# Two blocks on one core: the first block's attention regrouped into four rounds of head pairs

## The chip, the core and the metric

One core of a Trainium2 chip runs the whole program. The metric is the device time of one execution in microseconds. Everything is in fp32. The profile shows every matmul product as two records, so a product of two accumulation steps appears as four records. Engines are named as in the profile: PE is TensorE (PEld its weight loads), DVE is VectorE, ACT is ScalarE, POOL is GpSimd and SP is SyncE, whose queue issues the weight loads.

## What is computed

Two model blocks run one after the other on 256 tokens of width 1024. Block 1 has two layers, each with a convolution branch, a neighbourhood attention with 8 heads of 64 channels, an output projection and a feed-forward part (dense in layer 0, eight experts with two chosen per token in layer 1). Block 2 has two layers of windowed attention and a recurrent part, and is steered by a condition vector. Only this part of the reference bears on the change:

```python
# block 1, layer i
conv_out = conformer_conv(a, g, conv_w[i], conv_b[i], conv_ln_g[i], conv_ln_b[i])
attn_out = neighbourhood_attention(q, k, v, rpb[i])   # per head: softmax(q k^T * scale + bias, masked) v
mix = jnp.concatenate([conv_out, attn_out], axis=-1) @ w_out[i] + b_out[i]
h = layer_norm(DEEPNORM_ALPHA * h + mix, ln1_g[i], ln1_b[i])
# block 2, layer l: its modulation depends on the conditions alone
mod_x = jnp.split((sc @ w_ada[l] + b_ada[l])[:, None, :], 3, axis=-1)
mod_c = jnp.split(scc @ w_ada[l] + b_ada[l], 3, axis=-1)
```

The condition product `sc @ w_ada[l]` needs nothing of block 1, so the kernel computes it beside block 1's attention.

## The kernel before

Each engine has its own program, written out by hand, and semaphores order them. Activations are kept with features on partitions and 256 tokens on the free axis. Weights come as 471 units of 1 MB each (128 partitions by 2048 numbers), loaded by SP in the order of use into a ring of six slots. A slot is loaded again when TensorE has released its unit: `next_unit` waits for a unit and, unless it is called with `beside=True`, marks all units held so far for release; the next product (`mm`, L463) carries the release. A unit taken `beside` others is held together with them.

PSUM has eight banks of 512 numbers per partition. `fill` (TensorE) waits until the bank's last reader is done; `tile` (the readers) waits until the bank is full.

One layer of block 1 is: projection (10 units), then the attention stage, then `block1_out` (the attention half of the output projection, 2 units), then the norm and the feed-forward part. In layer 1 the experts follow; which experts' units are loaded is read from the routing's result by SP.

The attention stage mixes four kinds of work on TensorE.

- A condition row (`condition_row`): one unit of `w_ada`, eight products with a stationary operand of 32 columns in four column groups, 256 columns moving. ScalarE copies the row out of PSUM (L1556) into `cond_row`, which has two places. Layer 0 has 12 rows, layer 1 has 8.
- A turn of a row (`condition_turn`): two products with two moving columns, which sum the four groups and put the row on partitions. It waits for ScalarE's copy.
- Attention: the scores of head i are two products with 64 rows of the array (L627), head i in row half i % 2 and bank 2 + i % 2. VectorE adds bias and mask (L2148) and takes the negative maximum (L2151), ScalarE takes the exponentials (L1635) and their sums, VectorE scales by the reciprocal sum (L2137, L2139), TensorE transposes the weights (L641, four transposes), ScalarE copies them (L1629), and TensorE multiplies by the values (L650): two products with 64 columns, head h in column half h % 2 of bank 6. ScalarE copies a pair's output (L1626). `prob1` has three places, `pt1` two.
- The convolution half of the output projection (`conv_half`): 8 output chunks, each of four accumulated products of full width into bank 7. ScalarE reads each with a bias (L1640), VectorE adds the residual (L2155). One unit holds the weights of four chunks.

In the loop over i, TensorE does: row i + 3 and turn of row i + 2, scores of head i, chunk i - 1, transposes of head i - 2, output of head i - 3. Three rows come ahead of the loop. ScalarE's Silu of the convolution branch (L1617), which the chunks need, stands behind its three row copies. `mixed_order` gives the order of the units of rows and chunks, from which the host lays out the weights.

Of the kernel before, what the change touches and what calls it, by code (L numbers as in the profile page):

```python
# [108 lines left out]

def mixed_order(l):  # L110

    rows = [("row", u) for u in range(l * ADA_EARLY, UNITS_ADA)]
    order, rows = rows[:4], rows[4:]
    for i in range(1, HEADS + 1):
        order += rows[:1]
        rows = rows[1:]
        if i % 4 == 1:
            order.append(("half", i // 4))
    return order + rows
# [66 lines left out]
def build(nc, weights, params, consts, x_t, ctx_t, p_t, rel, out):  # L186
    with ExitStack() as ctx:
# [50 lines left out]
        prob1, pt1 = cut(3, TT, T), cut(2, TT, T)  # L238
# [4 lines left out]
        cond_s = cut(KC, 32)  # L243

# [191 lines left out]
        def _(eng):  # L436
# [130 lines left out]
            half_open = [False]  # L567

            def condition_row(l, u, bank):
                w = next_unit(beside=half_open[0])  # L570
                o = fill(("row", l, u), bank, (s["cond_row"], UNITS_ADA * l + u + 1))
# [3 lines left out]
                last.then_inc(bank_full[bank], 1)  # L575

            def condition_turn(l, u, mod_t):
                eng.wait_ge(s["cond_row"], UNITS_ADA * l + u + 1)
                for half in range(2):
                    at = 2 * (2 * u + half)  # L580
                    last = mm(mod_t[:, at:at + 2], cond_row[:, u % 2, half * P:half * P + P],
                              con[:, CN("fold", 0, 2)], True, True)
                return last

            def conditions(l):


                eng.wait_ge(s["cond_ready"], 1)
                mod_t = fill(("mod", l), 0, (s["mod_out"], 2 * l + 1))
                for u in range(l * ADA_EARLY, UNITS_ADA + 1):  # L590
                    if u < UNITS_ADA:
                        condition_row(l, u, 1)
                    if u > l * ADA_EARLY:
                        last = condition_turn(l, u - 1, mod_t)
                    if u == UNITS_ADA:
                        last.then_inc(bank_full[0], 1)
                    yield
# [15 lines left out]
            def block1_attention(l, filler):  # L613
                eng.wait_ge(s["qk_out"], CC * (l + 1))
                eng.wait_ge(s["v_out"], 2 * (l + 1))
                for i in range(HEADS + 3):
                    half_open[0] = 1 <= i <= HEADS and i % 4 != 1
                    if i % 4 == 2 and half_open[0]:
                        release[0] += held[0] - 1
                        held[0] = 1  # L620
                    before_row = unit_no[0]
                    next(filler, None)
                    if i < HEADS:
                        b, p0 = 2 + i % 2, DH * (i % 2)
                        o = fill(("s", l, i), b, (s["nbr_scored"], HEADS * l + i + 1))
                        for t in range(TT):
                            last = mm(o[:, t * T:(t + 1) * T], q1[p0:p0 + DH, i // 2, t * P:t * P + P],  # L627
                                      k1[p0:p0 + DH, i // 2, :], True, True)
                        last.then_inc(bank_full[b], 1)
                    if 1 <= i <= KC:  # L630
                        if i % 4 == 1:
                            w = next_unit(beside=unit_no[0] > before_row)
                        conv_half(l, i - 1, w)
                    if 2 <= i < HEADS + 2:
                        h = i - 2
                        b = 4 + h % 2
                        eng.wait_ge(s["nbr_prob"], HEADS * l + h + 1)
                        o = fill(("pt", l, h), b, (s["nbr_turned"], HEADS * l + h + 1))
                        for t in range(TT):
                            for kt in range(TT):  # L640
                                last = eng.transpose(o[:, kt * T + t * P:kt * T + t * P + P],  # L641
                                                     prob1[:, h % 3, t, kt * P:kt * P + P], ident)
                        last.then_inc(bank_full[b], 1)
                    if i >= 3:
                        h = i - 3
                        eng.wait_ge(s["nbr_turned"], HEADS * l + h + 1)
                        if h % 2 == 0:
                            o2 = fill(("o", l, h // 2), 6, (s["nbr_out"], CC * l + h // 2 + 1))
                        for kt in range(TT):
                            last = mm(o2[DH * (h % 2):DH * (h % 2) + DH, 0:T],  # L650
                                      v1[:, kt, h * DH:h * DH + DH], pt1[:, h % 2, kt, :], kt == 0, kt == TT - 1)
                        if h % 2 == 1:
                            last.then_inc(bank_full[6], 1)

            def conv_half(l, c, w):

                if c == 0:
                    eng.wait_ge(s["conv_mixed"], CC * (l + 1))
                o = fill(("half", l, c), 7, (s["mix_biased"], KC * l + c + 1))
                for k in range(CC):  # L660
                    at = k * 4 * P + (c % 4) * P
                    last = mm(o[:, 0:T], w[:, at:at + P], mix1[:, k, :], k == 0, k == CC - 1)
                last.then_inc(bank_full[7], 1)
# [774 lines left out]
            for l in range(DEPTH):  # L1438
                block1_projection(l)
                filler = conditions(l)  # L1440
                for _ in range(3):
                    next(filler)
                block1_attention(l, filler)
                for _ in filler:
                    pass
# [88 lines left out]
        def _(eng):  # L1534
# [23 lines left out]
            def conditions(l):  # L1558
                for u in range(l * ADA_EARLY, UNITS_ADA):
                    condition_row(l, u)  # L1560
                    yield
# [58 lines left out]
            def block1_attention(l, filler):  # L1620
                for i in range(HEADS + 4):
                    next(filler, None)
                    if i >= 5 and i % 2 == 1:
                        h2 = (i - 5) // 2
                        o = tile(eng, "o", l, h2)
                        eng.activation(mix1[:, CC + h2, :], o[:, 0:T], ACT.Copy).then_inc(s["nbr_out"], 1)  # L1626
                    if 3 <= i < HEADS + 3:
                        o = tile(eng, "pt", l, i - 3)
                        eng.activation(pt1[:, (i - 3) % 2].rearrange("p a b -> p (a b)"), o, ACT.Copy)\  # L1629
                            .then_inc(s["nbr_turned"], 1)  # L1630
                    if i < HEADS:
                        k = HEADS * l + i + 1
                        eng.wait_ge(s["nbr_max"], k)
                        for t in range(TT):
                            eng.activation(prob1[:, i % 3, t, :], prob1[:, i % 3, t, :], ACT.Exp,  # L1635
                                           bias=rmax[:, i % 3, t:t + 1], accum_out=rsum[:, i % 3, t:t + 1])\
                                .then_inc(s["nbr_exp"], 1)
                    if 1 <= i <= KC:
                        o = tile(eng, "half", l, i - 1)
                        eng.activation(sq[:, i - 1, :], o[:, 0:T], ACT.Identity, bias=par[:, PC(f"b_out{l}", i - 1)])\  # L1640
                            .then_inc(s["mix_biased"], 1)
# [316 lines left out]
            for l in range(DEPTH):  # L1958
                block1_projection(l)
                filler = conditions(l)  # L1960
                norm(f"conv{l}", CC, T)
                for _ in range(3):
                    next(filler)
                conv_silu(l)
                block1_attention(l, filler)
                for _ in filler:
                    pass
# [30 lines left out]
        def _(eng):  # L1998
# [132 lines left out]
            def block1_attention(l):  # L2131
                eng.wait_ge(s["rel_ready"], TT * (l + 1))
                for i in range(HEADS + 2):
                    if i >= 2:
                        h = i - 2
                        eng.wait_ge(s["nbr_exp"], 2 * (HEADS * l + h + 1))
                        link(eng.reciprocal(rinv[:, h % 3, :], rsum[:, h % 3, :]))  # L2137
                        for t in range(TT):
                            ins = eng.tensor_scalar(prob1[:, h % 3, t, :], prob1[:, h % 3, t, :],  # L2139
                                                    rinv[:, h % 3, t:t + 1], None, ALU.mult)  # L2140
                        ins.then_inc(s["nbr_prob"], 1)
                    if i < HEADS:
                        k = HEADS * l + i + 1
                        pr = prob1[:, i % 3]
# [959 lines left out]
```

## Time and profile before

| | us |
|---|---|
| median of the runs shown (3) | 2128.38 |
| lowest and highest | 2126.7, 2137.03 |
| the profiled execution | 2130.35 |
| its span, first to last instruction | 2128.6 |
| attention stage of layer 0, first row to `block1_out` (96.49 to 152.03) | 55.54 |
| attention stage of layer 1 (498.96 to 548.72) | 49.76 |

Times in the rows are microseconds from the start of the span. In a row of the order of time stand the start, the length of a merged run of equal instructions, the engine, the line, the operation, the tiles, the shape and the count; in brackets how long the engine was idle before it and what ended that. A merged run's length reaches to its last record's end, which overlaps the start of the next run, so the cost of a run on TensorE is read from its start to the next run's start.

### The profile page before, as it was taken

What the parts mean: (1) busy time and instruction counts of PE and PEld (TensorE: products, weight loads), DVE (VectorE), ACT (ScalarE), POOL (GpSimd) and SP (SyncE); (2) the same over time, 40 slices, a digit from 0 to 9 for tenths busy, and PEclk for the clock granted to TensorE, in tenths of its full rate; (3) what the DMA queues carried; (4) which work ended last, traced back from release to release, by engine and by line L of the source; (5) the groups of instructions that cost most, each with busy time, mean ns of one, the idle gap of its engine ahead of it and who ended that gap; (6) DMA issues with size and microseconds to landing.
All of it is one profiled execution on the core that took longest, in us unless ns stands there. A gap on an engine that the chain in (4) does not pass through costs nothing.

```text
span 2128.6 us, 36866 instructions
## 1 busy us (share of the span) xinstructions
PE 2036.4 (96%) x15858; PEld 1470.3 (69%) x15858; DVE 790.8 (37%) x1796; ACT 406.6 (19%) x964; POOL 5.7 (0%) x12
## 2 busy tenths in 40 slices
PE   8999999999999999999999999998999999999887
PEld 6879999987776656666666566665744667474776
DVE  5737555595521111111011101112336354346454
ACT  1232110103310111000000000001133333023322
POOL 0000000000000000000000000000000000000000
PEclk9999999999999999999999999999999999999999
DMA  9464445444189999999999999995211111131120
GB/s 316 175 242 176 159 165 193 176 176 163 47 349 390 420 420 417 420 420 420 421 418 420 420 419 418 420 414 231 79 60 40 60 40 40 60 119 60 40 80 20
DMA packets 72372, 506.74 MB, mean 238 GB/s; under 512 B 7824, under 2 KB 9872, under 8 KB 11792
## 3 DMA queue, kind: packets, MB, share of 16 engines
q1 hardware_dynamic: 71056, 500.15, 58.6%
q0 software_dynamic: 1152, 4.19, 0.9%
q8 instruction: 128, 2.10, 0.4%
q14 instruction: 36, 0.29, 0.0%
HBM read 503.27 MB, written 1.05 MB: 237 GB/s over the span
## 4 chain that ended last, share of the span: by engine, by line
PE 87%; DMA 6%; DVE 3%; ACT 2%; issue 1%; SPq 0%; DVEq 0%; ACTq 0%
PE ps L463 85%; DMA work<-weights 4%; DMA ring<-weights 2%; PE ps L1225 1%; PE ps L778 1%; DVE work L2696 1%; ACT work L1844 0%; DMA xc<-x_t 0%; DVE work L2657 0%; PE ps L641 0%; DVE work L2763 0%; DVE work L2653 0%; PE ps L1326 0%; DVE work L2654 0%; ACT work L1617 0%
## 5 line engine op out<-in xcount | busy, mean ns | idle before, releaser
L463 PE MATMUL ps<-work 128*32 128x256 f32 (+8 forms) x5608 | 585.5, 382 | 22.7 <-DVE work L2708 6.3
L463 PE MATMUL ps<-work,ring 128*128 128x256 f32 (+2 forms) x2056 | 525.6, 409 | 7.2 <-DVE work L2763 5.0
L463 PEld LDWEIGHTS ps<-work 128*32 128x32 f32 (+3 forms) x5608 | 378.7, 138 | 187.4 <-issue 110.3
L463 PE MATMUL ps<-ring,work 128*32 128x256 f32 (+3 forms) x4824 | 469.0, 410 | 13.5 <-DMA work<-weights 3.8
L463 PEld LDWEIGHTS ps<-work,ring 128*128 128x128 f32 x2056 | 350.9, 191 | 149.2 <-issue 111.9
L463 PEld LDWEIGHTS ps<-ring,work 128*32 128x32 f32 (+1 forms) x4824 | 260.1, 119 | 147.7 <-issue 76.3
L463 PE MATMUL ps<-xc,ring 128*128 128x256 f32 (+1 forms) x1440 | 276.6, 352 | 5.6 <-DMA ring<-weights 4.0
L463 PEld LDWEIGHTS ps<-xc,ring 128*128 128x128 f32 x1440 | 241.4, 191 | 42.4 <-issue 6.7
L2309 DVE TENSOR_TENSOR work<-work,ps 128x256 f32<-128x256 f32 x42 | 17.7, 422 | 421.0 <-ACT work L1688 421.0
L463 PE MATMUL ps<-xc,work 128*128 128x256 f32 (+1 forms) x720 | 138.3, 350 | 0.0
L463 PEld LDWEIGHTS ps<-xc,work 128*128 128x128 f32 x720 | 120.8, 191 | 19.9 <-issue 3.8
L1688 ACT ACTIVATE work<-ps 128x256 f32<-128x256 f32 x42 | 16.2, 385 | 576.5 <-PE ps L463 576.5
L2083 DVE SCALAR_TENSOR_TENSOR work<-work,par 128x256 f32<-128x256 f32 x240 | 98.0, 486 | 0.9
L2271 DVE TENSOR_TENSOR work<-ps,work 128x512 f32<-128x512 f32 x68 | 47.1, 692 | 92.3 <-PE ps L463 92.0
L463 PE MATMUL ps<-work,con 128*128 128x256 f32 x230 | 58.1, 399 | 11.7 <-ACT work L1546 5.6
L463 PEld LDWEIGHTS ps<-work,con 128*128 128x128 f32 x230 | 44.1, 198 | 24.2 <-issue 11.9
L2430 DVE TENSOR_TENSOR work<-ring 128x512 f32<-128x512 f32 x52 | 33.6, 688 | 51.6 <-PE ps L463 51.6
L463 PEld LDWEIGHTS ps<-con,work 128*128 128x128 f32 x336 | 42.4, 190 | 13.3 <-issue 8.2
L463 PE MATMUL ps<-con,work 128*128 128x128 f32 (+2 forms) x336 | 45.0, 267 | 2.8 <-DVE work L2654 2.8
L2323 DVE TENSOR_TENSOR work<-work 128x512 f32<-128x512 f32 x14 | 9.7, 692 | 97.6 <-ACT work L1696 97.6
L2609 DVE SCALAR_TENSOR_TENSOR work<-work,par 128x512 f32<-128x512 f32 (+1 forms) x64 | 39.8, 679 | 0.0
L1734 ACT ACTIVATE work<-ps 128x256 f32<-128x256 f32 x52 | 20.0, 384 | 103.1 <-PE ps L463 103.1
(277 smaller groups left out, 1186.0 us busy)
## 6 DMA issues: line engine op xcount, KB each, us to landing
ring<-weights SPq DMA_DIRECT2D x317, 1024.0 KB, 13.0
work<-weights SPq DMA_DIRECT2D x154, 1024.0 KB, 16.6
work<-rel POOLq DMA_DIRECT2D x8, 512.0 KB, 7.8
con<-consts SPq DMA_DIRECT2D x1, 1368.0 KB, 21.6
xc<-x_t SPq DMA_DIRECT2D x1, 1024.0 KB, 7.8
xc<-ctx_t SPq DMA_DIRECT2D x1, 1024.0 KB, 26.1
out<-work SPq DMA_DIRECT2D x4, 256.0 KB, 2.1
par<-params SPq DMA_DIRECT2D x1, 872.0 KB, 9.2
```

The costliest lines, as they stand in the source:

```text
L463: ins = eng.matmul(o, lhs, rhs, start=start, stop=stop, **kw)
L778: last = eng.transpose(o[:, k * P:k * P + P], pair_a[:, n % 2, k * P:k * P + P], ident)
L1225: last = eng.transpose(o[:, kt * P:kt * P + P], prob2_flat[:, at:at + P], ident)
L1688: eng.activation(pair_s[:, n % 2, :], o[:, 0:GW], ACT.Silu).then_inc(s["pair_silu"], 1)
L1734: eng.activation(snap[n % 2][:, at:at + T], o[:, 0:T], ACT.Copy).then_inc(s["snap_out"], 1)
L2083: ins = eng.scalar_tensor_tensor(out=conv_acc[:, j, :], in0=src, scalar=w, in1=conv_acc[:, j, :], op0=ALU.mult, op1=ALU.add)
L2271: return eng.tensor_tensor(r, o.rearrange("p (a b) -> p a b", b=T), r, ALU.add)
L2309: eng.tensor_tensor(pair_a[:, n % 2, :], pair_s[:, n % 2, :], o[:, GW:2 * GW], ALU.mult)\
L2323: eng.tensor_tensor(v, v, rows(gate_row, 2), ALU.mult).then_inc(s["first_weighted"], 1)
L2430: ins = eng.tensor_tensor(up_sum(i, z), in0, in1, op)
L2609: ins = eng.scalar_tensor_tensor(out=acc, in0=src, scalar=w, in1=acc, op0=ALU.mult, op1=ALU.add)
L2696: ins = eng.scalar_tensor_tensor(out=state[:, n, :], in0=state[:, n, :], scalar=wt_pair[:, j % 2, 1, n:n + 1], in1=o[:, h * 129:h * 129 + ...
```

## The change

The loop over 8 heads becomes a loop over four rounds of two heads.

- Scores: for each of the two query tiles the two heads' products alternate, head 2r in row half 0 and bank 2, head 2r + 1 in row half 1 and bank 3.
- Outputs: for each key tile the two heads' products alternate in the two column halves of bank 6.
- Rows: two units fill the two halves of one bank, ScalarE copies both with one instruction of 512 columns, and the turns of two rows follow each other. `cond_row` and a new `other_row` alternate. `ROW_ROUNDS` says in which rounds rows are drawn: ahead of the loop (-1), in rounds 0 to 3 and behind the loop (4) in layer 0; at -1, 0, 2 and 4 in layer 1.
- Chunks: two output chunks fill one bank (`half_pair`).
- `prob1` has two places in place of three. A pair's scores, softmax and transposes lie in one round, its output in the next.
- ScalarE's first row copy stands behind the Silu. TensorE's first turns stand behind the first scores and the second rows.

The order on TensorE in round r: scores of pair r, output of pair r - 1, two rows (where drawn), in round 0 the first turns, two chunks, two turns (where drawn), transposes of pair r. After round 3: two rows, the last output, the last turns.

The diff, cut to its core:

```diff
-            def conditions(l):
-                eng.wait_ge(s["cond_ready"], 1)
-                mod_t = fill(("mod", l), 0, (s["mod_out"], 2 * l + 1))
-                for u in range(l * ADA_EARLY, UNITS_ADA + 1):
...
+            def condition_rows(l, n, beside=False):
+                u = l * ADA_EARLY + 2 * n
+                bank = 1 if n else 5
+                o = fill(("row", l, u), bank, (s["cond_row"], UNITS_ADA * l + u + 2))
+                for k in range(2):
+                    w = next_unit(beside=beside or k == 1)
+                    for c in range(KC):
+                        at = 32 * (c % 4)
+                        last = mm(o[at:at + 32, k * GW:(k + 1) * GW], cond_s[:, c, :], w[:, c * GW:(c + 1) * GW],
+                                  c < 4, c >= KC - 4)
+                last.then_inc(bank_full[bank], 1)
...
-            def block1_attention(l, filler):
+            def block1_attention(l):
+                eng.wait_ge(s["cond_ready"], 1)
+                condition_rows(l, 0)
                 eng.wait_ge(s["qk_out"], CC * (l + 1))
                 eng.wait_ge(s["v_out"], 2 * (l + 1))
...
+                for r in range(HEADS // 2 + 1):
+                    drawn = ROW_ROUNDS[l].index(r) if r in ROW_ROUNDS[l] else None
+                    if r == HEADS // 2:
+                        condition_rows(l, drawn)
+                    if r < HEADS // 2:
+                        for k in range(2):
+                            h = 2 * r + k
+                            fill(("s", l, h), 2 + k, (s["nbr_scored"], HEADS * l + h + 1))
+                        for t in range(TT):
+                            for k in range(2):
+                                p0 = DH * k
+                                last = mm(ps[:, 2 + k, t * T:(t + 1) * T], q1[p0:p0 + DH, r, t * P:t * P + P],
+                                          k1[p0:p0 + DH, r, :], True, True)
+                                if t == TT - 1:
+                                    last.then_inc(bank_full[2 + k], 1)
+                    if r:
+                        eng.wait_ge(s["nbr_turned"], HEADS * l + 2 * r)
+                        o2 = fill(("o", l, r - 1), 6, (s["nbr_out"], CC * l + r))
+                        for kt in range(TT):
+                            for k in range(2):
+                                h = 2 * r - 2 + k
+                                last = mm(o2[DH * k:DH * k + DH, 0:T], v1[:, kt, h * DH:h * DH + DH], pt1[:, k, kt, :],
+                                          kt == 0, kt == TT - 1)
+                        last.then_inc(bank_full[6], 1)
+                    if r % 2 == 1:
                         release[0] += held[0] - 1
                         held[0] = 1
...
+                    if drawn is not None and r < HEADS // 2:
+                        condition_rows(l, drawn, beside=r % 2 == 1)
+                    if r == 0:
+                        mod_t = fill(("mod", l), 0, (s["mod_out"], 2 * l + 1))
+                        condition_turns(l, 0, mod_t)
+                    if r < HEADS // 2:
+                        if r % 2 == 0:
+                            w = next_unit(beside=drawn is not None)
+                        half_pair(l, r, w)
+                    if drawn is not None:
+                        condition_turns(l, drawn, mod_t)
...
+                o = fill(("half", l, r), 7, (s["mix_biased"], KC * l + 2 * r + 2))
+                for f in range(2):
+                    for k in range(CC):
+                        at = k * 4 * P + (2 * (r % 2) + f) * P
+                        last = mm(o[:, f * T:f * T + T], w[:, at:at + P], mix1[:, k, :], k == 0, k == CC - 1)
                 last.then_inc(bank_full[7], 1)
```

On ScalarE a round is: output copy of the pair before, exponentials of two heads, one copy of two rows (where drawn), two biased chunks, two copies of transposed weights. On VectorE a round is: bias and maximum of two heads, then reciprocal and scaling of two heads, then two residual additions.

## Rows read from the trace of the kernel before

**Rows 1.** Stretches (both stages): busy PE, PEld, DVE, ACT, POOL; clock, DMA, GB/s

```profile
96.49:152.03 55.54, 53.85 (x401) 35.92 (x400) 23.01 (x54) 26.21 (x70) 2.72 (x4) 1.00 0.69 243
498.96:548.72 49.76, 47.70 (x322) 32.19 (x321) 22.68 (x54) 24.76 (x66) 0.00 (x0) 1.00 0.44 170
```

**Rows 2.** Order of time on PE: one iteration of layer 0's loop

```profile
132.50 1.07 PE L463 MATMUL ps<-ring,work 128*32 128x256 f32 x16
133.50 0.61 PE L463 MATMUL ps<-con,work 128*128 128x2 f32 x4
134.03 1.13 PE L463 MATMUL ps<-work 64*128 64x256 f32 x4
135.09 1.99 PE L463 MATMUL ps<-work,ring 128*128 128x256 f32 x8
136.92 0.60 PE L641 MATMUL ps<-con,work 128*128 128x128 f32 x4
137.45 1.08 PE L463 MATMUL ps<-work 128*64 128x256 f32 x4
138.46 1.07 PE L463 MATMUL ps<-ring,work 128*32 128x256 f32 x16
```

**Rows 3.** PE's order of time: idles in layer 0's prologue and layer 1

```profile
98.16 1.07 PE L463 MATMUL ps<-ring,work 128*32 128x256 f32 x16 [0.59 <-ACT work L1556]
...
105.13 1.07 PE L463 MATMUL ps<-ring,work 128*32 128x256 f32 x16 [1.00 <-ACT work L1556]
...
547.22 1.56 PE L463 MATMUL ps<-work 128*64 128x256 f32 x8 [0.38 <-ACT work L1629]
```

**Rows 4.** Stretches: weights in layer 0's stage and at layer 1's routing

```profile
130.00:140.00 10.00, 10.00 (x75) 6.56 (x73) 4.07 (x11) 4.19 (x14) 0.00 (x0) 1.00 1.00 424
...
575.00:580.00 5.00, 5.00 (x37) 4.63 (x36) 2.26 (x10) 0.90 (x2) 0.00 (x0) 1.00 0.00 0
...
585.00:590.00 5.00, 2.28 (x5) 1.85 (x6) 4.76 (x19) 0.07 (x1) 0.00 (x0) 0.50 1.00 398
```

**Rows 5.** PE's order of time in block 2's attention: row halves, column halves

```profile
1556.86 1.13 PE L463 MATMUL ps<-work 64*128 64x512 f32 x4 [0.19 <-ACT work L1780]
1557.92 3.70 PE L463 MATMUL ps<-work,ring 128*128 128x512 f32 x8
...
1671.01 1.09 PE L463 MATMUL ps<-work 128*64 128x128 f32 x16
```

**Rows 6.** Groups of weight loads by form, layer 0's stage: busy us, mean ns

```profile
L463 PEld LDWEIGHTS ps<-work 128*64 128x64 f32 x32 | 3.7, 136 | 2.6 <-issue 1.0 <-ACT work L1629 0.2
```

**Rows 7.** Order of time on VectorE in layer 0's stage

```profile
98.89 1.43 DVE L2033 TENSOR_TENSOR work<-work 128x256 f32<-128x256 f32 x4
...
129.24 0.69 DVE L2148 TENSOR_TENSOR work<-ps,work 128x512 f32<-128x512 f32 x1 [3.49 <-PE ps L463]
129.96 0.69 DVE L2151 TENSOR_REDUCE small<-work 128x2 f32<-128x512 f32 x1
...
131.09 0.62 DVE L2139 TENSOR_SCALAR work<-work,small 128x256 f32<-128x256 f32 x2
```

**Rows 8.** Order of time on ScalarE in layer 0's stage

```profile
101.34 1.28 ACT L1617 ACT_TABLE_LOAD   x1
102.64 2.08 ACT L1617 ACTIVATE work<-work,par 128x256 f32<-128x256 f32 x4
...
128.22 0.60 ACT L1629 ACTIVATE work<-ps 128x512 f32<-128x512 f32 x1
...
130.68 0.51 ACT L1635 ACTIVATE work<-work,small 128x256 f32<-128x256 f32 x1 [1.86 <-DVE small L2151]
```

**Rows 9.** DMA view, 90 to 165 us: queue and issues (median to landing)

```profile
q0 software_dynamic: 576, 2.10, 13.0%
...
ring<-weights SPq DMA_DIRECT2D x16, 1024.0 KB, 7.6
```

**Rows 10.** Order of time on GpSimd from 95 to 165 us

```profile
142.15 2.72 POOL L1530 DMA_DIRECT2D work<-rel  x4 [105.47 <-DVE work L2148]
```

More of the change, by code:

```diff
@@ L107, in moe_order @@
             yield GATES, EARLY_GATES + GATE_CELLS.index(c)
+ROW_ROUNDS = ([-1, 0, 1, 2, 3, 4], [-1, 0, 2, 4])
 def mixed_order(l):
[L112 to L119, printed above, removed]
+    order, u = [], l * ADA_EARLY
+    for r in range(-1, HEADS // 2 + 1):
+        if r in ROW_ROUNDS[l]:
+            order += [("row", u), ("row", u + 1)]
+            u += 2
+        if r in (0, 2):
+            order.append(("half", r // 2))
+    assert u == UNITS_ADA
+    return order
 def ring_places():
@@ L565, in block1_projection, with row_products @@
                 norm_var(f"conv{l}", CC, T, True, 2)
[L567 to L571, printed above, removed]
+            def row_products(l, u, o):
+                w = next_unit()
                 for c in range(KC):
@@ L574, in condition_row, with turn @@
                     last = mm(o[at:at + 32, 0:GW], cond_s[:, c, :], w[:, c * GW:(c + 1) * GW], c < 4, c >= KC - 4)
-                last.then_inc(bank_full[bank], 1)
+                return last
+            def condition_row(l, u, bank):
+                o = fill(("row", l, u), bank, (s["cond_row"], UNITS_ADA * l + u + 1))
+                row_products(l, u, o).then_inc(bank_full[bank], 1)
+            def turn(u, rows, mod_t):
+                for half in range(2):
+                    at = 2 * (2 * u + half)
+                    last = mm(mod_t[:, at:at + 2], rows[:, u % 2, half * P:half * P + P],
+                              con[:, CN("fold", 0, 2)], True, True)
+                return last
@@ L577, in condition_turn @@
             def condition_turn(l, u, mod_t):
                 eng.wait_ge(s["cond_row"], UNITS_ADA * l + u + 1)
[L579 to L583, printed above, removed]
-            def conditions(l):
-                eng.wait_ge(s["cond_ready"], 1)
-                mod_t = fill(("mod", l), 0, (s["mod_out"], 2 * l + 1))
-                for u in range(l * ADA_EARLY, UNITS_ADA + 1):
[L591 to L597, printed above, removed]
+                return turn(u, cond_row, mod_t)
@@ L630, in block1_attention @@
[L630 to L653, printed above, removed]
@@ L1439, in _ @@
                 block1_projection(l)
[L1440 to L1445, printed above, removed]
+                block1_attention(l)
                 block1_out(l)
@@ L1556, in condition_row, with condition_rows @@
                 eng.activation(cond_row[:, u % 2, :], o[:, 0:GW], ACT.Copy).then_inc(s["cond_row"], 1)
[L1558 to L1561, printed above, removed]
+            def condition_rows(l, n):
+                u = l * ADA_EARLY + 2 * n
+                o = tile(eng, "row", l, u)
+                eng.activation(row_of[n % 2].rearrange("p a b -> p (a b)"), o, ACT.Copy).then_inc(s["cond_row"], 2)
             def context_squares():
@@ L1959, in _ @@
                 block1_projection(l)
[L1960 removed]
                 norm(f"conv{l}", CC, T)
[L1962 to L1963 removed]
                 conv_silu(l)
[L1965 to L1967 removed]
+                condition_rows(l, 0)
+                block1_attention(l)
                 norm(f"ln1_{l}", KC, T)
```

125 lines of the change are left out of this document (67 added, 58 removed).

## Prediction, made before the changed kernel was run

> **What bounds the kernel now.** I read the table of stretches over the two attention stages first, then TensorE in order of time inside them, then the helpers in the same order, then the weight stream. The two stages (block 1's layers 0 and 1) last 55.54 and 49.76 us; TensorE is busy 53.85 and 47.70 of that at full clock, VectorE 23.01 and 22.68, ScalarE 26.21 and 24.76, and the DMA engines 0.69 and 0.44 of the time [rows 1]. The order of time shows the same: in the steady loop every TensorE group starts where the one before it ends, and one iteration takes 138.46 - 132.50 = 5.96 us [rows 2]. From the starts, a condition row costs 1.00, its turn 0.53, a head's scores 1.06, an output chunk 1.83, the four transposes 0.53, a head's output 1.01. So TensorE's own length is the bound here, helpers have slack, and what shortens TensorE's list shortens the program. The exceptions are the idle times: 0.59 and 1.00 us in layer 0's prologue behind ScalarE's copy of a row, the same two in layer 1, and 0.38 before layer 1's last output [rows 3].
>
> Time gained here reaches the end. The expert weights cannot be asked for before the routing: the stream stands still and then fills the DMA engines from 585 us on [rows 4]. So it moves with its start, and so does all that follows.
>
> **Scores on row halves.** The count of products stays. Before, a head's two products are four records that use 64 of 128 rows, one after the other, 1.06 us [rows 2]. After, the two heads of a pair alternate, each in its own row half and its own bank. The trace has this form already, in block 2: two products of 64x512 in the two row halves take 1.06 us to the next start (1556.86 to 1557.92), in four records, while eight full-width records of 128x512 behind them take 3.70 [rows 5]: 0.27 against 0.46 each. Halves therefore run side by side. A pair costs what one head costs: 8 heads x 1.06 become 4 x 1.06 in each layer, -4.24 us a layer.
>
> **Outputs on column halves.** Again block 2 has the form: 16 records of 128*64 on 128 columns take about 1.09 us, 0.07 each [rows 5], against 0.13 each for the full-width transposes on 128 columns (4 in 0.53) [rows 2]. So a pair should cost one head's 1.01: 8 x 1.01 become 4 x 1.01. The last two heads already ran one behind the other without a change of form, 1.50 for both in layer 1 (547.22 to the stage's end) [rows 1, 3], so the gain is 6 x 1.01 + 1.50 - 4 x 1.01 = 3.5; I take -3.6 us a layer, since layer 0's last pair is longer.
>
> One rule speaks against this half. The rows that bear on it: a load of 128*64 takes 136 ns by itself [rows 6], and yet in block 2 the records of such pairs follow each other every 0.07 us, loads included [rows 5]. The Trainium skill ("TensorE: Matmul & The Clock Gate", The mechanism) says that a weight load overlaps a running matmul only when the row groups differ, and column halves share all rows. By that rule each of 4 load steps a round would lie bare, 4 x 0.136 x 8 rounds = 4.4 us of the gain gone; the rows say otherwise, and I leave it a small chance.
>
> **Fewer changes of form.** A group loses some time at its start and end. One record step is 0.216 us in a chunk of 8 (1.83 = 8 x 0.216 + 0.10) and about 0.11 in turns and transposes. Two units in one row group cost 2 x 1.00 - 0.13, two turns 2 x 0.53 - 0.09, two chunks 3.66 - 0.10, two heads' transposes 1.06 - 0.09. Six row pairs in layer 0 and four in layer 1, with four rounds each, give -2.1 and -1.6 us. Bounds: nothing, if the wait for the second unit splits the group as before, to these sums; I take them, since waits already met cost no gap in the steady loop [rows 2].
>
> **The prologue.** Before, three single rows each wait for ScalarE's copy. After, TensorE runs rows (1.87), the first pair's scores (1.06), rows (1.87), and only then the turns. ScalarE now does Silu first. VectorE's four scaled chunks are there from 99.3 to 100.32 [rows 7]; the Silu table load (1.28) was issued only at 101.34 behind the third copy and can now lie beside VectorE's work; four Silu take 2.08 [rows 8]. That gives 99.35 + 2.08 = 101.4, then one copy of 128x512 at 0.60 [rows 8], 0.14 until TensorE starts: 102.1. TensorE arrives at 96.5 + 0.1 + 1.87 + 1.06 + 1.87 = 101.4. So 0.7 us of idle instead of 1.59; the same in layer 1. Bounds: 0.3 to 2.0 (the table load bare). The last output is covered by rows at the end (0.38 gone), but two rounds without rows in layer 1 may show 0.2 each at the output, behind ScalarE's two biased chunks and two copies. I take -0.8 us for each layer.
>
> **What hides the softmax.** The chain of a pair is now shut into one round, with two weight buffers in place of three. From the scores' end, VectorE adds and takes maxima for two heads, 4 x 0.69 = 2.8; the second head's two exponentials take 2 x 0.51; its scaling 0.62 with a reciprocal before it, 0.8; with hand-overs 4.85 us until the second head may be turned [rows 7, 8]. In front of those transposes TensorE has the previous output 1.0, two chunks 3.56 and the first head's transposes 0.5: 5.1. That covers it by 0.25 in the two rounds of layer 1 without rows, and by 3.1 where rows (1.87) and turns (0.97) are drawn. ScalarE's queue in a round is exponentials, row copy, two chunks, two transposed copies; the turns behind the row copy need it by S + 6.4 and get it by S + 4.5 (S: scores' end). So cost nothing, up to 1 us in each of two rounds.
>
> **The weight stream.** The loads behind SP's queue number the same, but units are released in twos and threes, at a row pair's first product. A unit of 1 MB takes about 2.5 us at 424 GB/s [rows 4], and 7.6 from issue to landing in the median, queue included [rows 9]; three released together have landed after about 3 x 2.5 + 2 = 9.5 us (the 2 is an estimate: 7.6 less two units ahead). A round lasts 9.44; the first two of them are due one round later, the third two. Tight spot: POOL's bias loads for layer 1 start when layer 0's last scores are read (142.15 before [rows 10], about 130 after). They hold 13.0% of a window of 75 us, 9.8 us [rows 9], and now share the engines with the two units for the last row and the first output unit. Slowed 1.9-fold, the latter lands about 139 to 141 and is due at 140.2. I take 0.5 us, bounds 0 to 3.
>
> **The sum.** Layer 0: 4.24 + 3.6 + 2.1 + 0.8 - 0.5 = 10.24; layer 1: 4.24 + 3.6 + 1.6 + 0.8 = 10.24. Together 20.5 us, so stages of 45.3 and 39.5 us. The profiled execution took 2130.35 us (span 2128.6 and 1.75 around it); less 20.5 it is 2109.9. The median of the runs shown is 2128.38, 2 lower, so I say 2108.0.
>
> **Rivals.**
> - Late weights: the joint releases leave TensorE waiting for a landing in three or four rounds of layer 0, 1 to 2 us each. For: the DMA engines were full in parts of the stage (424 GB/s) [rows 4]. Against: six slots, and 0.69 mean. 2110 to 2118.
> - The chain shows in the rounds without rows and in the first ones, 0.5 to 1 us each in 6 of 8: 2110 to 2114. The bare loads of the column halves would end in the same place: 20.5 - 4.4 = 16.1, 2112.
> - The halves don't run side by side here (two products of the same half in a row might hold the other back): scores and outputs gain nothing, 20.5 - 15.7 = 4.8: 2123.6. Against: the row and column pairs of block 2 [rows 5].
> - Slower: the helpers' chain becomes the round's length. ScalarE's one queue carries exponentials, row copies, chunks and transposed copies for TensorE; if the chunk product had to wait for the bias reads of the preceding round, its bank's one reader, TensorE's fill would stand behind the chain and not beside it. A round would be 1.06 + 4.85 + 0.97 + 1.3 + 1.0 + 1.87 + 3.56 + 0.97 = 15.6 us against 2 x 5.96 = 11.9, eight rounds +29, less 1.6 of prologue: 2156. It decides when ScalarE reaches those reads later than the next round's chunk; by my order of its queue it ends them about 1.0 us after a chunk (two reads, each of half the width of the 0.60 copy [rows 8]) and the next comes at least 4.5 later. The Trainium skill ("TensorEngine Tiling (Array Packing)", PSUM Bottleneck) warns that after tiling the PSUM copies may be what limits; ScalarE's 26.21 us in a stage of 45 [rows 1] keeps that away.
> - More gain: the prologue idles vanish and the groups' edges shrink further: 2099 to 2103.
>
> **How the numbers follow.** Forecast 0.73 (own range 2103 to 2112), late weights 0.07, the chain 0.05, bare loads 0.02, halves not together 0.05, slower 0.04, more gain 0.04. The clock is full in both stages [rows 1], but 0.50 in a stretch at the routing [rows 4]; moving the program by 20 us may lengthen or shorten such stretches, some 2 us either way, which the range holds. The range 2101 to 2116 takes in the forecast and most of the first two rivals, and leaves out the others, 0.13 or so. A measurement of this kernel can tell about 0.5% (10.6 us) from no change: faster by more than that is all above except halves not together (0.05 to the same, with 0.02 of the latest weights) and slower: 0.89, 0.07, 0.04.
>
> **What would show it.** After: groups of 8 records of 64*128 in 1.06 us and of 128*64 in 1.0; row pairs of 32 records in 1.87; one idle of 0.7 in each prologue behind ScalarE's copy; hardly any between; the routing's idle moved 20 us forward and unchanged behind it. It would be wrong if those groups took 2 us, if TensorE idles before transposes behind VectorE in each round, or if it waits for DMA.

## The result

The changed kernel took 2111.15 us (median of 4 executions, 2109.45 to 2112.75), the kernel before 2132.7 us beside it (4 executions, 2126.7 to 2137.27): a ratio of 0.9901 with an interval of 0.9881 to 0.9921, so 21 us less. That is inside the forecast range, 3 us above the forecast time.

The profiled execution of the changed kernel took 2112.75 us, its span 2111.0, which is 17.6 less than the span before. The two attention stages, in the table of stretches (columns as in [rows 1]):

```profile
100.34:143.87 43.53, 42.83 (x401) 31.28 (x401) 22.93 (x53) 26.03 (x65) 2.77 (x4) 1.00 0.73 260
495.23:533.38 38.15, 37.44 (x321) 27.62 (x321) 22.89 (x53) 24.84 (x63) 0.00 (x0) 1.00 0.60 222
```

They are 12.01 and 11.60 us shorter than in [rows 1], with the same number of records on TensorE (401; 321 against 322) and the same work on VectorE and ScalarE. TensorE's order of time in layer 0's prologue and in one steady round (two runs of scores and outputs that follow each other are merged here, 16 records under the name of the first):

```profile
100.34 1.93 PE L469 MATMUL ps<-ring,work 128*32 128x256 f32 x32
102.21 1.13 PE L469 MATMUL ps<-work 64*128 64x256 f32 x8
103.27 1.93 PE L469 MATMUL ps<-ring,work 128*32 128x256 f32 x32
105.91 1.02 PE L469 MATMUL ps<-con,work 128*128 128x2 f32 x8 [0.70 <-ACT work L1587]
...
121.46 2.15 PE L469 MATMUL ps<-work 64*128 64x256 f32 x16
123.53 1.93 PE L469 MATMUL ps<-ring,work 128*32 128x256 f32 x32
125.40 3.72 PE L469 MATMUL ps<-work,ring 128*128 128x256 f32 x16
128.96 0.95 PE L469 MATMUL ps<-con,work 128*128 128x2 f32 x8
129.77 1.07 PE L681 MATMUL ps<-con,work 128*128 128x128 f32 x8
130.77 2.15 PE L469 MATMUL ps<-work 64*128 64x256 f32 x16
...
140.08 1.93 PE L469 MATMUL ps<-ring,work 128*32 128x256 f32 x32
141.94 1.08 PE L469 MATMUL ps<-work 128*64 128x256 f32 x8
142.96 1.05 PE L469 MATMUL ps<-con,work 128*128 128x2 f32 x8
143.87 7.15 PE L469 MATMUL ps<-work,ring 128*128 128x256 f32 x32
153.52 6.70 PE L469 MATMUL ps<-work,ring 128*128 128x256 f32 x22 [2.50 <-DMA ring<-weights]
```

A round takes 130.77 - 121.46 = 9.31 us, where two iterations took 2 x 5.96 in [rows 2]. Of the 2.6 us, 2.07 are the scores and outputs (2.07 for both, from 4.14), the rest edges of groups: rows 0.13, chunks 0.10, turns 0.25, transposes 0.06. The first pair's scores alone cost 1.06 (102.21 to 103.27), the last pair's output 1.02 (141.94 to 142.96), each for two heads.

The last row is the loss. Layer 0's output projection waits 2.50 us for its second unit of weights, where the kernel before ran its 64 records without a gap:

```profile
152.03 14.08 PE L463 MATMUL ps<-work,ring 128*128 128x256 f32 x64
```

In the changed kernel GpSimd's bias loads for layer 1 start 33.9 us after the stage's start (45.7 in the kernel before [rows 1, 10]), ahead of that unit, which is asked for at 140.73:

```profile
134.24 2.77 POOL L1556 DMA_DIRECT2D work<-rel  x4 [96.93 <-DVE work L2169]
```

The chain of work that ended last names the load, and the table of stretches behind it a lower granted clock:

```profile
140.73 12.75 DMA ring<-weights
```

```profile
145.00:150.00 5.00, 5.00 (x25) 4.38 (x25) 1.91 (x5) 0.00 (x0) 0.00 (x0) 1.00 1.02 253
150.00:155.00 5.00, 2.50 (x9) 1.84 (x8) 1.07 (x3) 0.00 (x0) 0.00 (x0) 0.88 1.02 296
155.00:160.00 5.00, 5.00 (x19) 4.16 (x19) 1.70 (x4) 0.00 (x0) 0.00 (x0) 0.78 1.01 400
```

The unit is the first of three asked for together and took 12.75 us, where the forecast reckoned 2.5 us for a unit and a latency of about 2; the DMA engines are full (1.02) but move only 253 to 296 GB/s. Then TensorE, which had idled 2.5 us, runs part of the next stretches at the lower of its two clocks (1.2 of 2.4 GHz, so the mean falls to 0.88 and 0.78). From the stage's end to the first products on the next norm's squares this costs 20.85 us where it was 16.42 before: 4.4 us given back. Of these 1.7 are the clock (the unit's 32 records take 8.70 us, 153.52 to 162.22, where they take 7.01 in runs that stay at full clock), the rest is the wait.

So the profiled spans differ by: stages -12.01 and -11.60, layer 0's output projection +4.43, the part behind layer 1's stage -2.27, and the start +3.85. The last two are not the change's. Behind layer 1's stage both kernels do the same, and in the eleven profiles on record that part took from 1576.4 to 1583.0 us, with the kernel before (1579.9) in the middle. Before the first attention stage both kernels do the same too, but this execution had a lower clock in its first 25 us:

```profile
10.00:15.00 5.00, 5.00 (x16) 3.75 (x14) 0.00 (x0) 0.00 (x0) 0.00 (x0) 0.66 1.01 423
15.00:20.00 5.00, 2.61 (x6) 2.15 (x7) 3.44 (x15) 4.34 (x10) 0.00 (x0) 0.73 1.01 423
```

The kernel before had 1.00 in both stretches of its profiled execution. Starts of 96.5 to 100.3 us until the first attention stage were seen among all the profiles, for kernels that are equal up to there. What this pair of profiles shows of the change itself is thus 12.01 + 11.60 - 4.43 = 19.2 us.

### The profile page after: what moved, and what is told of

It is laid out like the page before. It is cut to its first block, busy times and chain, and to the rows that moved or that the text cites. A ratio compares the mean times of both kernels' runs of the same rounds, so it can differ in the third digit from the quotient of the medians.

```text
span 2111.0 us, 36869 instructions
## 1 busy us (share of the span) xinstructions
PE 2019.2 (96%) x15858; PEld 1462.9 (69%) x15858; DVE 791.4 (37%) x1796; ACT 405.9 (19%) x954; POOL 5.9 (0%) x12
## 4 chain that ended last, share of the span: by engine, by line
PE 89%; DMA 4%; DVE 4%; ACT 2%; issue 1%; DVEq 0%; SPq 0%; ACTq 0%
PE ps L469 87%; DMA work<-weights 2%; DMA ring<-weights 2%; PE ps L1256 1%; PE ps L809 1%; DVE work L2724 1%; ACT work L1877 0%; DMA xc<-x_t 0%; DVE work L2685 0%; PE ps L681 0%; DVE work L2056 0%; DVE work L2791 0%; DVE work L2681 0%; PE ps L1357 0%; DVE work L2682 0%
## 5 line engine op out<-in xcount | busy, mean ns | idle before, releaser
L469 PE MATMUL ps<-work 128*32 128x256 f32 (+8 forms) x5608 | 570.8, 383 | 21.1 <-DVE work L2736 6.3
L469 PEld LDWEIGHTS ps<-work 128*32 128x32 f32 (+3 forms) x5608 | 369.9, 138 | 186.0 <-issue 109.7
L2637 DVE SCALAR_TENSOR_TENSOR work<-work,par 128x512 f32<-128x512 f32 (+1 forms) x64 | 39.8, 680 | 0.0
```

The lines of the kernel that those rows point to most:

```text
L469: ins = eng.matmul(o, lhs, rhs, start=start, stop=stop, **kw)
L2637: ins = eng.scalar_tensor_tensor(out=acc, in0=src, scalar=w, in1=acc, op0=ALU.mult, op1=ALU.add)
```

## The experiments

Two theories were open on the gain, and two on the loss. On the gain: products in different halves of the array run side by side when the kernel alternates them; or the gain is something else that came with the regrouping. On the loss: GpSimd's bias loads for layer 1, which now start earlier, take the DMA engines from the weights; or units are asked for too late because they are released in threes. Stage lengths below are read in each run's own trace, from the first row product to the first product of the output projection; the changed kernel has 43.53 and 38.15.

**The changed kernel again.**

> The changed kernel again, beside the runs that follow on the same chip. Expected 2109 to 2113 us. Of interest is what varies between executions: the stages should be 43.5 and 38.2 us again, and the first output projection should wait for its second unit of weights again (2.5 us).

Measured: 2108.67 us (6 executions, 2102.95 to 2115.69), ratio 0.9881 (0.9860 to 0.9901) to the kernel before on this chip (2132.58 us). Stages 44.13 (with one gap of 0.5 us that the trace puts to nothing) and 38.14; the wait for the unit 2.0 us, and the stretch from the stage's end to the norm's squares 20.33 us, 3.9 more than before. The loss is there in both profiles of the change, and in the five runs below that leave the bias loads and the condition rows as the change has them the wait is 1.8 to 2.5 us.

**Bias loads later.**

```diff
-                    eng.wait_ge(s["nbr_scored"], HEADS * l)
+                    eng.wait_ge(s["ffn_act"], 2)
                 for r in range(ROWS):
```

> The changed kernel, but GpSimd's bias loads for layer 1 start in the middle of layer 0's feed-forward part, not right behind layer 0's last scores. Theory (the bias loads take the DMA engines from the weights): the 2.5 us wait of layer 0's output projection for its second unit goes, and so does the stretch at half clock behind it, together 4 us: about 2107 us; both stages keep 43.5 and 38.2 us. Rival (the unit is asked for too late, because three units are released together): the wait stays at 1.5 to 2.5 us and the time at 2110 to 2111.

Measured: 2103.62 us (5 executions, 2102.79 to 2104.69), ratio 0.9866 (0.9844 to 0.9887). (The 2107 expected started from 2111.15; from the 2108.67 of this chip it would be 2104.7.) The bias loads start at 220 us. TensorE's order of time in the output projection, and the stretch from the stage's end to the norm's squares:

```profile
139.41 1.05 PE L469 MATMUL ps<-con,work 128*128 128x2 f32 x8
140.33 14.06 PE L469 MATMUL ps<-work,ring 128*128 128x256 f32 x64
154.22 1.38 PE L469 MATMUL ps<-work,con 128*128 128x256 f32 x4
```

```profile
140.33:156.73 16.40, 15.19 (x71) 12.76 (x70) 7.17 (x19) 0.56 (x2) 0.00 (x0) 1.00 0.81 343
```

All 64 records run through, at full clock, and the stretch is back at 16.40 us (16.42 in the kernel before). The release in threes is still there, so the bias loads were needed for the wait. In the DMA view of the same 75 us the median from issue to landing of the weights falls from 8.4 to 6.9 us:

```profile
ring<-weights SPq DMA_DIRECT2D x17, 1024.0 KB, 8.4
work<-rel POOLq DMA_DIRECT2D x4, 512.0 KB, 15.8
```

```profile
ring<-weights SPq DMA_DIRECT2D x17, 1024.0 KB, 6.9
```

```profile
work<-rel POOLq DMA_DIRECT2D x4, 512.0 KB, 7.8
```

The first fence is the changed kernel, the second this one, the third the bias loads in the kernel before. The bias loads themselves took 15.8 us in the median, against 7.8 in the kernel before: both sides lose. The median is 5 us under the changed kernel's; the single executions touch (2102.95 lies among these).

**Bias loads later, first turns behind the first chunks.**

```diff
                         mod_t = fill(("mod", l), 0, (s["mod_out"], 2 * l + 1))
-                        condition_turns(l, 0, mod_t)
...
                         half_pair(l, r, w)
+                    if r == 0:
+                        condition_turns(l, 0, mod_t)
```

> As the run before, and TensorE's first turns stand behind the first two chunks instead of ahead of them. Theory (the 0.7 us idle in each prologue is ScalarE's Silu and copy, which the chunks can cover): the idle shrinks to about 0.25 us, now before the chunks and ended by the Silu, so each stage is 0.5 us shorter, 43.0 and 37.7 us: about 2106 us. Rival (TensorE is in front of ScalarE there whatever it does): the idle stays 0.7 and only its place changes.

Measured: 2105.68 us (6 executions, 2104.33 to 2110.73), ratio 0.9881 (0.9860 to 0.9901). In the trace it does what was expected: stages 43.15 and 37.77, and TensorE's idle in the prologue falls to 0.33 and now ends with the Silu:

```profile
103.61 3.69 PE L469 MATMUL ps<-work,ring 128*128 128x256 f32 x16 [0.33 <-ACT work L1644]
```

0.75 us in all is less than these runs can tell (the medians stand the other way round by 2 us). The lowest median on record is that of the version with only the bias loads moved.

**Scores head by head.**

```diff
-                        for t in range(TT):
-                            for k in range(2):
+                        for k in range(2):
+                            for t in range(TT):
                                 p0 = DH * k
```

> The changed kernel, but the four score products of a pair in the old order: both of the first head, then both of the second. Theory (only neighbouring products in different row halves run side by side): one of four products still overlaps its neighbour, so a pair takes 7 record steps instead of 4, 1.8 us instead of 1.06: +0.65 to 0.75 in each of four rounds, stages of 46.3 and 41.0 us, about +5.5 us in all. Rival (the array sorts the halves out by itself, and the gain came from fewer groups): stages unchanged.

Measured: stages of 43.54 and 38.15 us (2107.75 us, one execution). Nothing changed. TensorE's order of time, the first pair's scores:

```profile
99.36 1.14 PE L469 MATMUL ps<-work 64*128 64x256 f32 x8
100.44 1.93 PE L469 MATMUL ps<-ring,work 128*32 128x256 f32 x32
```

1.08 us for eight records, as with alternation (1.06). The rival's number came out (its reason, fewer groups, is tested two runs further on), and the prediction's reason fell in part: alternating the heads is not what makes the halves run side by side.

**Outputs head by head.**

```diff
-                        for kt in range(TT):
-                            for k in range(2):
+                        for k in range(2):
+                            for kt in range(TT):
                                 h = 2 * r - 2 + k
```

> The changed kernel, but the four output products of a pair in the old order, head by head. Theory: as in the run before, 1.7 us instead of 1.02 for a pair: +0.65 to 0.75 in each of four rounds, stages of 46.3 and 41.0 us. Rival (weight loads of column halves lie bare, so alternating gains little): +0.2 a round, stages of 44.3 and 39.0.

Measured: stages of 43.54 and 38.16 us (2112.31 us, one execution), the last pair's output 1.02 us:

```profile
139.86 1.09 PE L469 MATMUL ps<-work 128*64 128x256 f32 x8
140.88 1.05 PE L469 MATMUL ps<-con,work 128*128 128x2 f32 x8
```

The same again for column halves. Neither the theory (+0.7 a round) nor the rival of bare weight loads (+0.2) came out.

**The heads' scores parted.** A new theory follows from the two runs: what counts is that the two heads' products are neighbours in TensorE's list, in whatever order. In the kernel before, a chunk, transposes, an output, a row and a turn stood between two heads' scores.

```diff
+                        scores(r, 0)          # head 2r: both products
+                        if r == 0:
+                            scores(r, 1)
...
                         last.then_inc(bank_full[6], 1)   # the preceding pair's output
+                        if r < HEADS // 2:
+                            scores(r, 1)
```

> The changed kernel, but in rounds 1 to 3 the preceding pair's output stands between the scores of the two heads. Theory (products in different halves run side by side when they are neighbours in the list, whatever their order within the pair; a group of another form between them parts them): the two heads cost 2 x 1.06 again, +1.06 in each of three rounds: stages of 46.7 and 41.3 us. Rival (the halves' products are sorted out across other groups too, and only the number of groups counts): +0.2 to 0.3 a round, 44.3 and 39.0 us.

Measured: stages of 46.88 and 41.30 us (2114.01 us, one execution), +3.35 and +3.15. Scores, output and scores of a round now take 3.13 us (2.07 before), without a wait:

```profile
505.08 3.20 PE L469 MATMUL ps<-work 64*128 64x256 f32 x16
508.21 3.72 PE L469 MATMUL ps<-work,ring 128*128 128x256 f32 x16
```

The same 16 records, 1.06 us more, with nothing changed but their neighbours. This is the gain's cause for the scores. The outputs were not parted in a run. For them it is inferred from their equal behaviour and from one place of the kernel before: the outputs of layer 1's last two heads stand next to each other in its list, head by head, and took 1.50 us for both [rows 3] instead of 2 x 1.01, although the second head's could start only when ScalarE had copied its weights, at 546.58 + 1.08 = 547.66, 0.44 us after the first:

```profile
546.58 1.08 ACT L1629 ACTIVATE work<-ps 128x512 f32<-128x512 f32 x2
```

The prediction put that difference down to the missing change of form; but from 547.66 to the stage's end is 1.06 us, about a head's output alone, so what was left of the first head's ran beside it.

**One chunk a bank.**

```diff
-                o = fill(("half", l, r), 7, (s["mix_biased"], KC * l + 2 * r + 2))
                 for f in range(2):
+                    o = fill(("half", l, r, f), 7, (s["mix_biased"], KC * l + 2 * r + f + 1))
...
-                last.then_inc(bank_full[7], 1)
+                    last.then_inc(bank_full[7], 1)
```

> The changed kernel, but each output chunk fills the bank by itself, so that the second chunk waits until ScalarE has read the first. Theory (two chunks a bank take ScalarE's queue out of TensorE's way): 0.75 us of idle in a round where ScalarE is free by then, 1.6 to 1.8 us where it is still at the exponentials (round 0, and the two rounds without rows in layer 1): layer 0 +3.8 to 47.3, layer 1 +5.9 to 44.0 us. Rival (ScalarE is always in time): at most +1 in each stage.

Measured: stages of 47.57 and 43.73 us (2117.48 us, one execution), within 0.3 us of the theory. TensorE's order of time in rounds 0 and 1 of layer 0:

```profile
103.14 1.97 PE L469 MATMUL ps<-work,ring 128*128 128x256 f32 x8
106.39 1.99 PE L469 MATMUL ps<-work,ring 128*128 128x256 f32 x8 [1.28 <-ACT work L1668]
...
113.98 1.99 PE L469 MATMUL ps<-work,ring 128*128 128x256 f32 x8
116.54 1.99 PE L469 MATMUL ps<-work,ring 128*128 128x256 f32 x8 [0.56 <-ACT work L1668]
```

The wait is longer where ScalarE is still at the exponentials. The idle shown (3.0 us in layer 0, 4.6 in layer 1) is less than the stages' growth, since a run's modelled end reaches into the gap behind it.

**The condition units one by one.**

```diff
-                o = fill(("row", l, u), bank, (s["cond_row"], UNITS_ADA * l + u + 2))
                 for k in range(2):
+                    o = fill(("row", l, u + k), bank, (s["cond_row"], UNITS_ADA * l + u + k + 1))
...
+                    last.then_inc(bank_full[bank], 1)
```

(On ScalarE, one copy of 256 columns for each row.)

> The changed kernel, but the two units of a row pair fill the bank one after the other, so that the second waits until ScalarE has copied the first. Theory (pairing the units keeps TensorE out of ScalarE's queue, where the copy stands behind the Silu and the exponentials): about +4 us ahead of the loop, +3.4 in round 0, +2.6 in each later round with rows, +0.7 behind the loop: layer 0 near 59, layer 1 near 49 us, so all of layer 0's gain is gone. Rival (the pairing only saves edges of groups): +0.13 a pair, 44.3 and 38.7 us.

Measured: stages of 68.06 and 53.46 us (2147.63 us, one execution beside 2136.37 of the kernel before). The direction is the theory's, the size more than its 59 and 49. The waits are the expected ones, 14.4 us in layer 0 and 9.0 in layer 1 behind ScalarE's copy:

```profile
PE ps L469 <- ACT work L1588: 14.4, 6, 4.2
```

and the lower clock is about the size of the surplus: a mean of 0.85 over 68.06 us is 10 us, and the 43.53 of the changed kernel with 14.4 and 10 comes to 68 (in layer 1 the mean is 0.87). The stretches of this run (the stage, and its first part) and TensorE's order of time there:

```profile
97.14:165.20 68.06, 53.63 (x402) 36.75 (x401) 22.93 (x53) 27.13 (x71) 2.77 (x4) 0.85 0.53 181
100.00:120.00 20.00, 14.45 (x79) 9.38 (x80) 5.11 (x13) 6.85 (x17) 0.00 (x0) 0.66 0.38 144
```

```profile
110.27 1.94 PE L469 MATMUL ps<-ring,work 128*32 128x256 f32 x16 [3.15 <-ACT work L1588]
112.14 1.87 PE L469 MATMUL ps<-con,work 128*128 128x2 f32 x8
113.87 6.67 PE L469 MATMUL ps<-work,ring 128*128 128x256 f32 x16
```

The two chunks that take 3.56 us at full clock took 6.5 (113.87 to 120.37) behind waits of 4.2 and 3.2 us. Pairing the units is thus no matter of saved edges: with the softmax shut into one round, a row that waits for ScalarE waits for the softmax.

**A longer chain.**

```diff
-                        eng.tensor_reduce(rmax[:, h % 4, :], pr, AX.X, ALU.max, negate=True).then_inc(s["nbr_max"], 1)
+                        link(eng.tensor_reduce(rmax[:, h % 4, :], pr, AX.X, ALU.max, negate=True))
+                        eng.tensor_reduce(rmax[:, h % 4, :], pr, AX.X, ALU.max, negate=True).then_inc(s["nbr_max"], 1)
```

> The changed kernel, with each head's maximum taken twice on VectorE, which makes a pair's chain about 1.5 us longer and changes no result. Theory (the chain is covered by 0.25 us in rounds without rows and by about 3 us where rows and turns are drawn): layer 0 stays at 43.5 us, layer 1 shows about 1.2 us in each of two rounds: 40.6 us. Rival (the chain is the round's length): +1.5 a round, 49.5 and 44.2 us.

Measured: stages of 43.53 and 40.81 us (2118.15 us, one execution). Layer 0 is the same to 0.01 us, layer 1 has its 2.66 us in the two rounds without rows. The waits there, and one round in TensorE's order of time:

```profile
PE ps L681 <- DVE work L2179: 1.8, 4, 0.6
```

```profile
506.50 3.72 PE L469 MATMUL ps<-work,ring 128*128 128x256 f32 x16
510.54 0.66 PE L681 MATMUL ps<-con,work 128*128 128x128 f32 x4 [0.32 <-DVE work L2179]
511.79 0.66 PE L681 MATMUL ps<-con,work 128*128 128x128 f32 x4 [0.60 <-DVE work L2179]
```

The chain grew by 1.44 us: in round 1 of layer 1 the second head's scaling ends 7.31 us after the round's first score, 5.87 in the changed kernel. So it is hidden much as worked out: the 1.44 us vanish where rows are drawn, and where they are not, only about 0.1 us of them does (1.33 show in each round).

## Why the prediction held, step by step

- **What bounds it.** Right: TensorE's list is the stages' length, before and after (42.83 busy of 43.53).
- **Scores and outputs.** The sizes were right (2.07 us for both in a round, forecast 1.06 + 1.01; the last output 1.02). (For block 2's 16 records the prediction took the merged length, 1.09 us; start to start, 1671.01 to 1672.03, they cost 1.02, which only strengthens its reading.) The reason was wrong in one part: the prediction put the gain to alternating heads, and held it possible that two products of the same half in a row hold the other back. Head by head gives the same stages to 0.02 us; parting the two heads' scores brings 1.06 us a round back. It is being neighbours that counts. The rule of the Trainium skill on bare weight loads ("TensorE: Matmul & The Clock Gate", The mechanism) would have shown as 0.5 us a round; the traces do not agree with it for column halves, which ran eight records in 1.02 us.
- **Fewer changes of form.** Right, but low for the turns: 0.81 us for two in a round (128.96 to 129.77) against 0.97 worked out. Over the ten row pairs the turns saved 2.6 us (11.07 before and 8.46 after, added up from the starts in both stages) against 0.9 worked out. Two heads' transposes take 1.00 against 0.97.
- **The prologue.** Right to the digit, and by the steps that were forecast (ScalarE's table load lies beside VectorE's work, TensorE waits for the copy behind the Silu): 0.70 us behind ScalarE's copy in layer 0, 0.71 in layer 1. The 0.2 us behind the transposed copies in the rounds without rows did not appear.
- **What hides the softmax.** Right: no wait in any round. The longer chain measured the cover: about 0.1 us in the rounds without rows, where 0.25 was forecast, and at least 1.44 elsewhere, where 3.1 was; how much more was not tried.
- **The weight stream.** The failed step. The 0.5 us taken (bounds 0 to 3) measured 4.4 and 3.9 us in the two profiles of the change: 2.50 and 2.0 us of wait, and a lower clock behind it. TensorE waiting for DMA was one of the prediction's own signs of being wrong. Two things were wrong in the working. It followed the first unit of the output projection, released at round 3, which was in time; the second, released behind the loop with two others, was the late one. And it priced the wait by TensorE's idle alone, without the clock behind it, which cost 1.7 us in four of the seven profiles that have the wait and nothing in the other three. The bias loads were rightly named as what the weights would meet. The median of 2111.15 also lies in the range of the late-weights rival, but what that rival said, waits in three or four rounds of layer 0, did not come: no round waited for a landing.
- **The sum.** Stages: 43.53 and 38.15 against 45.3 and 39.5 forecast, of which 0.5 was for the weights, so 2.6 us better: 1.7 of that are the turns, 0.55 the idle times. The weights were 3.9 us worse. That the total of 20.5 stands beside 19.2 in the profiles and 21.55 between the medians is in part luck, since these two misses have opposite signs. The forecast's range allowed the parts outside the stages some 2 us either way; in the profiles the part behind layer 1's stage varies by 6.5 us and the start by 3.9, whatever the kernel. Against the median that the forecast started from (2128.38 of three executions; 2132.7 with a fourth), the time itself came 3 us later than forecast.
- **The slower rival.** Nothing of it showed in the kernel as built. Kernels close to it lose much all the same, by waits that need only that one of the things that TensorE takes from ScalarE within a round is not paired. One chunk a bank costs 9.6 us in both stages together, single condition units 39.8, which is more than the 23.6 that the change gained there.

## What to carry to other kernels

In this kernel products that use half of the array's rows or columns gained when their partners stood next to them in the list; their order within that group made no difference here. Where a helpers' chain is shut into one round of an engine's list, look at whatever that engine takes from the same helpers in the round: here rows and chunks had to be buffered two at a time, or TensorE waited for ScalarE behind the chain. A stage that gets shorter moves up every load that is started by its progress: look up what those loads will meet, and price a wait of TensorE with and without a lower clock behind it.

## What the runs showed of the hardware that was not expected

- Products of two heads in one half each need not alternate: eight records took 1.08 us head by head and 1.06 alternating for row halves, 1.02 both ways for column halves.
- With the bias loads running, the DMA engines were full (1.02) at 253 to 296 GB/s in the two stretches shown, between an estimate of the bias loads' own rate (2.10 MB in 9.8 us, 214 GB/s [rows 9]) and the 424 of the weights [rows 4]; a weight load of 1 MB took 12.75 us.
- Seven profiles have the wait for the second unit of the output projection. Behind four of the waits (1.98, 2.30, 2.48 and 2.50 us) part of the next stretch ran at the lower clock, and the unit's 32 records took 8.70 us; behind the other three (1.79, 2.01 and 2.28 us) the clock stayed full and they took 7.01. The length of the wait alone does not decide: here are 2.30 us (one chunk a bank) and 2.28 us (scores head by head).

```profile
153.71 8.86 PE L469 MATMUL ps<-work,ring 128*128 128x256 f32 x32 [2.30 <-DMA ring<-weights]
```

```profile
150.48 7.17 PE L469 MATMUL ps<-work,ring 128*128 128x256 f32 x32 [2.28 <-DMA ring<-weights]
```

- Waits of 4.2 and 3.2 us lay in a stretch of 20 us at a mean clock of 0.66. Of two equal starts one had full clock and one 0.66 and 0.73. What decides between them was not tried.
